# Modulation steps moved from the input projection and the heads to the output projection of the mLSTM mixer, and the first head's scores ahead of the gate rows

## The reference, cut to what matters

```python
mod = silu(c) @ ada_w[i] + ada_b[i]              # 1024 -> 6144, for each layer
u = x * (1.0 + sc_m) + sh_m
xm, z = split(u @ w_in, 2)                       # 1024 -> 2 x 2048
xc = silu(causal_depthwise_conv(xm, conv_w, conv_b))
q, k, v = block_diag_proj(xc, wq), block_diag_proj(xc, wk), block_diag_proj(xm, wv)
gates = q @ wg_q + k @ wg_k + v @ wg_v + b_gates
h = mlstm(q, k, v, i_pre, log_sigmoid(f_pre))    # 4 heads of 512, causal scores with decay
h = (norm(h) * norm_w + skip * xc) * silu(z)
y = h @ w_out                                    # 2048 -> 1024
x = layer_norm(ALPHA * x + (1.0 + g_m) * y, ...)
```

## Time and profile before

| quantity | value |
|---|---|
| time, median of 3 runs | 2680.66 us (2680.2 to 2684.01) |
| the profiled execution's own time | 2685.28 us |
| its span, first to last instruction | 2683.5 us |
| mean granted TensorE clock | 0.993 |
| busy: PE, PEld, DVE | 2607.1, 1850.0, 897.3 us |
| busy: ACT, POOL | 418.4, 909.4 us |
| HBM read | 557.75 MB, 208 GB/s over the span |

### The profile page before, as it was taken

One profiled execution on the slowest core, in us unless ns is written; L12 is line 12 of the kernel. 1 busy time (PEld: TensorE's weight loads), 2 busy tenths in 40 slices (PEclk: granted clock), 3 DMA queues, 4 the chain that ended last, 5 costly groups with the idle time before them and its releaser, 6 DMA issues.

```text
span 2683.5 us, 47152 instructions
## 1 busy us (share of the span) xinstructions
PE 2607.1 (97%) x20611; PEld 1850.0 (69%) x20611; DVE 897.3 (33%) x1623; ACT 418.4 (16%) x864; POOL 909.4 (34%) x715
## 2 busy tenths in 40 slices
PE   8999999989999999999999999999999999999998
PEld 6767899947544444444445446488888888998998
DVE  5746431483300011100013494232221136533651
ACT  0032100120311000100003244110000031221000
POOL 2672178583000000000000360145555341622886
PEclk9999999999999999999999999999999999999999
DMA  9968544477499999999997210332222243123552
GB/s 300 342 237 298 142 166 166 151 282 256 164 382 407 408 384 385 394 399 406 383 388 269 75 47 10 102 110 88 85 87 87 79 141 110 49 78 97 171 166 87
DMA packets 318304, 561.88 MB, mean 209 GB/s; under 512 B 45545, under 2 KB 181521, under 8 KB 317969
## 3 DMA queue, kind: packets, MB, share of 16 engines
q1 hardware_dynamic: 299280, 554.57, 57.9%
q10 hardware_dynamic: 18816, 4.27, 0.8%
HBM read 557.75 MB, written 1.05 MB: 208 GB/s over the span
## 4 chain that ended last, share of the span: by engine, by line
PE 50%; issue 37%; POOLq 5%; POOL 4%; DVE 2%; ACT 1%; DMA 1%; DVEq 1%; SPq 0%; ACTq 0%
PE psum L1943 10%; PE psum L2230 5%; PE psum L2019 5%; PE psum L2053 3%; PE psum L1406 3%; PE psum L1021 3%; PE psum L2295 2%; PE psum L1359 2%; PE psum L2113 2%; PE psum L1768 2%; POOLq L3906 2%; PE psum L1419 1%; PE psum L2140 1%; POOLq L4046 1%; PE psum L1062 1%
## 5 line engine op out<-in xcount | busy, mean ns | idle before, releaser
L1629 PE MATMUL psum<-ring,xe 128*32 128x512 f32 (+1 forms) x4608 | 457.8, 557 | 1.0 <-issue 1.0
L1629 PEld LDWEIGHTS psum<-ring,xe 128*32 128x32 f32 x4608 | 156.7, 110 | 289.7 <-issue 254.8
L4045 POOL TENSOR_TENSOR ckv<-ckv,nstat 128x512 f32<-128x512 f32 x2 | 2.5, 1262 | 889.6 <-DVE nstat L3548 889.6
L3438 DVE TENSOR_TENSOR act_in<-act_in,psum 128x256 f32<-128x256 f32 (+1 forms) x72 | 28.7, 399 | 628.5 <-ACT act_in L2585 628.5
L1651 PE MATMUL psum<-ring,zs 128*32 128x256 f32 x4224 | 232.3, 379 | 0.3 <-DMA ring<-in_moe_w 0.3
L1651 PEld LDWEIGHTS psum<-ring,zs 128*32 128x32 f32 x4224 | 141.5, 110 | 93.0 <-issue 5.6
L4058 POOL TENSOR_TENSOR w_sums<-ring 128x512 f32<-128x512 f32 (+1 forms) x34 | 42.3, 1245 | 293.8 <-DVE ctxT L3605 124.1
L2585 ACT ACTIVATE act_in<-psum 128x256 f32<-128x256 f32 (+1 forms) x72 | 26.3, 366 | 566.7 <-PE psum L1629 566.7
L1768 PE MATMUL psum<-a,ring 128*128 128x512 f32 x224 | 96.8, 593 | 2.0 <-ACT a L2640 1.3
L3548 DVE RECIPROCAL nstat<-nstat 128x512 f32<-128x512 f32 x23 | 75.8, 3329 | 42.1 <-ACT nstat L2337 42.1
L1021 PE MATMUL psum<-a,ring 128*128 128x256 f32 x384 | 84.4, 380 | 0.4 <-DVE a L3806 0.3
(11 more groups left out here) (616 smaller groups left out, 4858.0 us busy)
## 6 DMA issues: line engine op xcount, KB each, us to landing
ring<-in_moe_w SPq DMA_DIRECT2D x216, 1024.0 KB, 11.2
ring<-in_ffn_w SPq DMA_DIRECT2D x97, 1024.0 KB, 5.2
ring<-in_ada_w SPq DMA_DIRECT2D x96, 1024.0 KB, 8.7
ring<-in_moe_w SPq DMA_DIRECT2D x64, 768.0 KB, 6.5
ring<-in_hg_w_in SPq DMA_DIRECT2D x20, 1024.0 KB, 5.1
ring<-in_mlstm_w_in SPq DMA_DIRECT2D x16, 1024.0 KB, 8.4
ring<-in_mlstm_w_out SPq DMA_DIRECT2D x8, 1024.0 KB, 7.5
ring<-in_s_w_glu SPq DMA_DIRECT2D x8, 1024.0 KB, 11.7
```

The source lines that it names most:

```text
L1629: last = pe.matmul(psum[rows, r, 0:2 * nb * 32].rearrange("p (u b f) -> p u b f", u=2, b=nb), xe[:, k, at:at + 32], tile[:, :, :, rows], s ...
```

## The change

The number of modulation steps beside the input tiles falls from 10 to 8 (tiles 5 to 12), so tiles 13 to 15 follow each other. Eight steps, 8 to 15, stand between there and the end of the heads (ten before): one behind the q and k products, one behind the first two gate rows, two in each of the first two heads, one in each of the last two. The last four, 16 to 19, stand behind the first four tiles of the output projection, and their loads between those tiles' loads. `ada_columns` moves behind the fifth output tile.

The first head's scores move ahead of the gate columns and rows. The gate rows of heads 2 and 3 move behind the first head's values, and ACT instead of DVE copies the rows of heads 1 to 3 out. ACT's last gate exponential moves ahead of the last two copies of v. On DVE `head_scale(h)` moves from the end of head h + 1 to behind the scores of head h + 2, and both last ones stand after the loop. `s5_loads` on ACT now follows `mod_rows_out("b")`. The hunks that only renumber banks are left out:

```diff
-UNDER_INPUT, FIRST_INPUT = 10, 6
+UNDER_INPUT, FIRST_INPUT, UNDER_OUTPUT = 8, 6, 4
...
-TILES += [(f"ada_b{UNDER_INPUT}", 20), ("m_out", 8), ("ffn0", 3 * FSTEPS), ("ada_c", 28), ("glu", 8), ("ada_r", 8),
+TILES += [(f"m_in{_j}", 1) for _j in range(FIRST_INPUT + UNDER_INPUT, INPUT_TILES)]
+TILES += [(f"ada_b{UNDER_INPUT}", 16)]
+for _s in range(UNDER_OUTPUT):
+    TILES += [(f"m_out{_s}", 1), (f"ada_out{_s}", 2)]
+TILES += [("m_out_rest", 8 - UNDER_OUTPUT), ("ffn0", 3 * FSTEPS), ("ada_c", 28), ("glu", 8), ("ada_r", 8),
...
-        ("m_v", 8), ("m_cT", 1), ("m_rows", NH), ("m_head", 4 * NH),
+        ("m_v", 8), ("m_head", 5 * NH + 1),
...
+        def head_job(kind, h):
+            later = 4 * h + 5 if h else 0
+            return job_of["m_head"] + {"scores": later, "cT": 1, "rows": (2, 3, 7, 8)[h], "sums": later + 1 if h else 4,
+                                       "values": later + 2 if h else 5}[kind]
...
-    for s in range(UNDER_INPUT, ADA_STEPS["b"]):
+    for s in range(UNDER_INPUT, ADA_STEPS["b"] - UNDER_OUTPUT):
...
-    t0 = tile_of["m_out"]
...
-        load_cols(t0 + j, w["mlstm_w_out"][0], 256 * (j % 4), 256, k0=8 * (j // 4))
+        load_cols(out_tile(j), w["mlstm_w_out"][0], 256 * (j % 4), 256, k0=8 * (j // 4))
+        if j < UNDER_OUTPUT:
+            ada_b(ADA_STEPS["b"] - UNDER_OUTPUT + j)
...
-    ada_step("b", UNDER_INPUT + 1, 1)
...
-    j = job_of["m_cT"]
+    def head_scores(h):
+        j = head_job("scores", h)
+        wait_free(pe, j)
+        for s in range(2):
+            for c in range(HC):
+                last = pe.matmul(key_block(bank(j), s), xc[:, h * HC + c, s * P:(s + 1) * P],
+                                 qk[:, h * HC + c, 0, s * P:T], start=c == 0, stop=c == HC - 1)
+        full(last, j)
+    def head_rows(h):
+        j = head_job("rows", h)
+        wait_free(pe, j)
+        full(pe.matmul(bank(j), ident[0:NH, h:h + 1].broadcast_to([NH, P]),
+                       gate_rows[0:NH, 5:7].rearrange("p a t -> p (a t)"), start=True, stop=True), j)
+    wait_out(pe, job_of["m_qk"] + IC - 1)
+    head_scores(0)
+    j = head_job("cT", 0)
...
-    for h in range(NH):
-        j = job_of["m_rows"] + h
-        wait_free(pe, j)
-        full(pe.matmul(bank(j), ident[0:NH, h:h + 1].broadcast_to([NH, P]),
-                       gate_rows[0:NH, 5:7].rearrange("p a t -> p (a t)"), start=True, stop=True), j)
+    for h in range(2):
+        head_rows(h)
+    ada_step("b", UNDER_INPUT + 1, 1)
...
-    wait_out(pe, job_of["m_qk"] + IC - 1)
...
-        j = job_of["m_head"] + 4 * h
-        wait_free(pe, j)
-        for s in range(2):
-            for c in range(HC):
-                last = pe.matmul(key_block(bank(j), s), xc[:, h * HC + c, s * P:(s + 1) * P],
-                                 qk[:, h * HC + c, 0, s * P:T], start=c == 0, stop=c == HC - 1)
-        full(last, j)
-        ada_step("b", UNDER_INPUT + 2 + 2 * h, 1)
+        if h:
+            head_scores(h)
+        ada_step("b", UNDER_INPUT + 2 + min(2 * h, h + 2), 1)
...
-        wait_out(pe, j)
-        wait_free(pe, j + 1)
+        j = head_job("sums", h)
+        wait_out(pe, head_job("scores", h))
+        wait_free(pe, j)
...
+        if h == 0:
+            for later in range(2, NH):
+                head_rows(later)
...
-        ada_step("b", UNDER_INPUT + 3 + 2 * h, 1)
-    ada_columns("b", 0, 1)
+        if h < 2:
+            ada_step("b", UNDER_INPUT + 3 + 2 * h, 1)
...
-            t, j = tile_of["m_out"] + 4 * half + g, job_of["m_out"] + g
+            t, j = out_tile(4 * half + g), job_of["m_out"] + g
...
-            elif g == 1:
-                head_var(NH - 1)
+                if g == 0:
+                    ada_columns("b", 0, 1)
+            else:
+                if g == 1:
+                    head_var(NH - 1)
+                ada_step("b", ADA_STEPS["b"] - UNDER_OUTPUT + g, 1)
...
+        if g == 6:
+            act.wait_ge(S("m_sum_ready"), 1)
+            act.activation(gate_rows[0:NH, 6], gate_rows[0:NH, 6], ACT.Exp, scale=-1.0).then_inc(S("gate_rows_ready"), 1)
...
-    act.wait_ge(S("m_sum_ready"), 1)
-    act.activation(gate_rows[0:NH, 6], gate_rows[0:NH, 6], ACT.Exp, scale=-1.0).then_inc(S("gate_rows_ready"), 1)
+    def rows_out(h):
+        j = head_job("rows", h)
+        wait_full(act, j)
+        out_of(act.activation(nm[:, h], bank(j).rearrange("p (k t) -> p k t", k=2), ACT.Copy), j)
...
+        if h == 0:
+            for later in range(1, NH):
+                rows_out(later)
...
-    mod_rows_out("b")
...
+    mod_rows_out("b")
...
-    for h in range(NH):
-        j = job_of["m_rows"] + h
-        wait_full(dve, j)
-        out_of(dve.tensor_copy(nm[:, h], bank(j).rearrange("p (k t) -> p k t", k=2)), j)
...
+        j = head_job("rows", h)
+        if h == 0:
+            wait_full(dve, j)
+            out_of(dve.tensor_copy(nm[:, h], bank(j).rearrange("p (k t) -> p k t", k=2)), j)
+            dve.drain()
+        else:
+            wait_out(dve, j)
...
+    decays(0)
...
-    decays(0)
...
+        if h >= 2:
+            head_scale(h - 2)
...
-        if h:
-            head_scale(h - 1)
+    head_scale(NH - 2)
+    head_scale(NH - 1)
...
-    head_scale(NH - 1)
```

More of the change, by code:

```diff
@@ L518, in ada_tile @@
             if stage == "b":
-                return tile_of[f"ada_b{s}"] if s < UNDER_INPUT else tile_of[f"ada_b{UNDER_INPUT}"] + 2 * (s - UNDER_INPUT)
+                if s < UNDER_INPUT:
+                    return tile_of[f"ada_b{s}"]
+                at_output = s - (ADA_STEPS["b"] - UNDER_OUTPUT)
+                return tile_of[f"ada_out{at_output}"] if at_output >= 0 else tile_of[f"ada_b{UNDER_INPUT}"] + 2 * (s - UNDER_INPUT)
             if stage == "c" and s >= ADA_BATCH["c"]:
@@ L1341, in stage_mlstm @@
                                 at = h * DH + (2 * g + e) * P
-                                last = pe.matmul(bank(j + 2 + g)[:, e * T + s * P:(e + 1) * T], vbuf[:, s, at:at + P],
+                                last = pe.matmul(bank(j + g)[:, e * T + s * P:(e + 1) * T], vbuf[:, s, at:at + P],
                                                  key_block(scor[:, h % 2], s), start=s == 0, stop=s == 1,
                                                  skip_group_check=True)
-                        full(last, j + 2 + g)
+                        full(last, j + g)
+                    if h == 0:
+                        for later in range(2, NH):
+                            head_rows(later)
                     if h:
                         head_var(h - 1)
-                    ada_step("b", UNDER_INPUT + 3 + 2 * h, 1)
-                ada_columns("b", 0, 1)
+                    if h < 2:
+                        ada_step("b", UNDER_INPUT + 3 + 2 * h, 1)
                 for half in range(2):
@@ L2446, in head_squares @@
             def head_squares(h):
-                wait_out(act, job_of["m_head"] + 4 * h + 3)
+                wait_out(act, head_job("values", h) + 1)
                 act.activation(hsq, hT[:, h * HC:(h + 1) * HC], ACT.Square).then_inc(S("h_sq_ready"), 1)
@@ L3125, in stage_mlstm @@
                     out_of(dve.scalar_tensor_tensor(scor[:, h % 2], bank(j)[:, 0:CAUSAL], DH ** -0.5, decay, ALU.mult, ALU.mult), j)
-                    wait_full(dve, j + 1)
-                    dve.tensor_tensor(recip_[:, 0], bank(j + 1)[:, 0:T], nm[:, h, 1], ALU.max)
+                    if h >= 2:
+                        head_scale(h - 2)
+                    j = head_job("sums", h)
+                    wait_full(dve, j)
+                    dve.tensor_tensor(recip_[:, 0], bank(j)[:, 0:T], nm[:, h, 1], ALU.max)
                     dve.drain()
-                    out_of(dve.scalar_tensor_tensor(recip_[:, 0], bank(j + 1)[:, 0:T], -1.0, recip_[:, 0],
-                                                    ALU.mult, ALU.max), j + 1)
+                    out_of(dve.scalar_tensor_tensor(recip_[:, 0], bank(j)[:, 0:T], -1.0, recip_[:, 0],
+                                                    ALU.mult, ALU.max), j)
                     dve.drain()
@@ L3134, in stage_mlstm @@
                     dve.drain()
+                    j = head_job("values", h)
                     for g in range(2):
-                        wait_full(dve, j + 2 + g)
+                        wait_full(dve, j + g)
                         out_of(dve.tensor_tensor(hT[:, h * HC + 2 * g:h * HC + 2 * g + 2],
-                                               bank(j + 2 + g).rearrange("p (a t) -> p a t", a=2),
-                                               recip_[:, 1:2].broadcast_to([P, 2, T]), ALU.mult), j + 2 + g)
+                                               bank(j + g).rearrange("p (a t) -> p a t", a=2),
+                                               recip_[:, 1:2].broadcast_to([P, 2, T]), ALU.mult), j + g)
                     if h + 1 < NH:
```

12 lines of the change are left out of this document (7 added, 5 removed).

## The result

| | before | after |
|---|---|---|
| median, us | 2681.73 (6 runs, 2679.05 to 2685.09) | 2693.74 (5 runs, 2692.29 to 2694.27) |
| profiled execution, us (span) | 2685.28 (2683.5) | 2693.82 (2691.9) |
| ratio, 95% interval | | 1.0042 [1.0031, 1.0052] |

One more execution of the change took 4688 us at a granted clock of 0.634, and is left out. The change is slower by 12.0 us by the medians and by 8 to 14 us by the interval; the forecast was 2674.2 us, and its range ended at 2679.0.

What follows compares the result with a forecast made beforehand. PE, busy 2607.1 of 2683.5 us, was taken as the bound, leaving only waits and half-clock time to win: 3.7 + 0.74 + 0.74 - 0.5 + 1.8 = 6.5 us, so 2680.7 - 6.5 = 2674.2 us, range 2669.5 to 2679.0.

Steps and rivals of the forecast that it cites:

- the last sentence on the output projection: Output projection: the next stage's small loads follow later on ACT, but are needed only in that stage; no cost.
- The rival on the slower side: Output projection starves: its tiles, slowed to 208 GB/s, make PE wait 14.5 us; 2688.7 us, chance 0.04.
- input projection, 7.86 less two steps: Input projection: both waits for POOL's weight sums go, and tiles beside steps no longer run longer; gain 3.7 us.
- zero product to output projection, columns and their wait taken out: Gate rows and heads: gain 0.74 us at the exponential, cost 0.5 for DVE and POOL, gain 1.8 on the clock.
- columns without the copy's wait: Modulation columns, moved behind the output projection's fifth tile, no longer wait for ACT's copy of the rows; gain 0.74 us.
- output projection with steps between its tiles: Output projection: steps 16 to 19 keep PE busy as in the heads and transfers keep up; no extra cost.
- to the layer norm: All terms together: gain 6.5 us, with the layer norm beginning at about 298.4 us instead of 304.80.
- the zero product: Sign: the first product behind the input tiles comes at about 159.2 us instead of 166.59.
- the gate rows' 0.74: Gate rows: PE no longer waits for ACT's exponential behind the values; gain 0.74 us.
- DVE and POOL ahead of the output projection: End of the heads: the output projection waits for DVE and POOL; cost 0.5 us, between 0 and 1.5.
- The forecast of the clock: Gate rows and first scores: a 5.2 us half-clock loss becomes two spells of 1.7 us; gain 1.8 us.
- the rival without a spell: Gate rows: no half-clock spell is left, all 5.2 us come back; -9.9 us, 2670.8 us, chance 0.22.

Runs made afterwards that it cites:

- experiment 2: The change with the time steps loaded as whole rows of 256 bytes (128 packets instead of 4,096): 2678.05 us, 0.9984.
- experiment 3: The change with time steps loaded as whole rows, plus both transfers of 4-byte packets as loads that nobody reads: 2696.05 us, 1.0044.
- experiment 4: The change with time steps loaded as whole rows, plus one of the two 4-byte-packet transfers as an unread load: 2677.96 us, 0.9977.
- `b_rows`: The kernel before the change, with the time steps loaded as whole rows: 2684.07 us, 0.9997.
- `b_loads_later`: The kernel before the change, its nine small loads held back on ACT until PE begins the output projection's fifth tile: 2692.54 us, 1.0038.
- experiment 7: The change with time steps as whole rows, and two moved modulation steps put back under the input projection: 2679.16 us, 0.9982.
- experiment 8: The change with time steps as whole rows, and the nine small loads issued ahead of ACT's copy of the modulation rows: 2695.81 us, 1.0058.
- experiment 6: Two kernels with time steps loaded as whole rows: the kernel before, 2684.07 us, 0.9997; the change once more, 2678.9 us, 0.9985.

## Why the prediction was wrong

**The step that failed** is the last sentence on the output projection: "`s5_loads` follow later on ACT, but are needed only in the next stage." It was costed at nothing. It asked who reads the data, and when; it did not ask what the transfers do to others while they run, nor how long they run. Both could be read in the trace of before: in the kernel before the two time-step loads take up to 46.4 us from issue to landing, and a stretch of 14 us has a DMA share of 0.06 with tiles of the ring issued. In the change the same packets went out 12.7 us later and PE came 7.8 us earlier, so that they were still running when PE stopped in the middle of a group: 12.7 us of stop and 2.2 at half clock (experiments 2, 3 and 4). The term of the sum that stood at 0 was a cost of 14.9 us. The rival on the slower side, a starved output projection, named the meeting of small loads and tiles, and ruled it out since the small loads "cannot meet these tiles". They met the last ones, but with the opposite effect: the tiles reached PE in time, with no wait for DMA there, and it was the small loads that were pushed back (12.27 us on the third).

**The other terms** came out near their sizes in this pair of executions. Between marks of the two traces, with the moved steps taken out at the prediction's own 1.85 us each:

| term | forecast | measured |
|---|---|---|
| input projection, 7.86 less two steps | +3.7 | +4.2 |
| zero product to output projection, columns and their wait taken out | +2.0 | +3.7 |
| columns without the copy's wait | +0.74 | +0.85 |
| output projection with steps between its tiles | 0 | -0.9 |
| to the layer norm | 6.5 | 7.8 |

The second row is 247.74 - 166.59 = 81.15 us before, less two steps and the columns with their wait (1.66), 75.8, against 230.82 - 158.73 = 72.1. The fourth is 297.00 - 230.82 = 66.2 us against 304.80 - 247.74 = 57.1, of which four steps are 7.4 and the columns 0.8.

- Input: both waits for POOL went from the last tiles, the zero product stood at 158.73 where 159.2 was forecast.
- The second term is the gate rows' 0.74, DVE and POOL ahead of the output projection (forecast 0.5, measured 0.78), and the clock. One spell came where two were taken: a window around it reads

```profile
185.00:190.00 5.00, 5.00 (x24) 1.17 (x26) 3.31 (x7) 1.28 (x3) 4.83 (x5) 0.66 0.10 11
```

(1 - 0.66) x 5 = 1.7 us lost. It lies behind the first two gate rows with no idle time of PE near it; the second pair of rows stayed at full clock. So a spell without a gap is there again, as the row from 192 to 204 us had shown it, but behind one piece, not two. The forecast of the clock, 1.8 us, came out as 5.2 - 1.7 = 3.5. The rule of the Trainium skill on idle gaps ("TensorE: Matmul & The Clock Gate", section "HAM oscillation — how this bites in real kernels") as the prediction read it would have given 5.2; the spell without a gap is no case of it.
- How much of the 3.5 is the change? The mixer's code on PE is the same in several of the kernels, so their traces are more samples of it. From 175 to 215 us the granted clock is 0.87, 0.91 and 0.96 in three executions with the order of before (before, `b_rows`, `b_loads_later`): 5.2, 3.6 and 1.6 us lost. In eight with the change's order, or two steps off it (experiment 7), it is 0.96 in three (the change, experiments 7 and 8) and 1.00 in five. So the spell is no fixed cost of the products that use 4 of 128 rows, against what the prediction took from the rows of before, and the profiled execution of before had the longest: the prediction took 5.2 us for what every execution loses, where the mean of three is 3.5. The gain by these means is 2.9 us, between the 1.8 of the forecast and the 3.5 of the pair. In the five at 1.00 the whole spell is gone, as the rival without a spell had it.
- The same holds for the lead at the layer norm. It begins at 304.80, 303.11 and 300.00 us in the three with the order of before, and at 297.00, 296.18, 296.42, 296.17 and 295.74 in the change and four executions (experiments 2, 6, 3 and 4) that differ from it only behind that point: 6.3 us apart on average, where the one pair has 7.8 and the forecast was 6.5. That the forecast of the lead is this close is in part luck, as the errors of its terms offset each other.
- The output projection's tiles take 7.10 us each beside steps, 0.07 more than before, and each step another bit at its edges: a small cost that I had set at zero, as I had counted the same thing as a gain under the input projection.

**How much of it arrives** could be told only with the small packets gone: about 4 us by the ratios of two comparisons, between 1.6 and 7.0 by their intervals. The forecast 6.5 lies at the upper end of that, and no version had a median near 2674.2 us. Where the rest of the lead at the layer norm goes was not followed.

## What to carry to other kernels

Moving work past a queue of small loads is not free because their data is needed late: ask how many packets they are, how long those run, and which tiles and instruction blocks are due while they do. A load whose rows are single elements with a stride can be made a load of whole rows, and picked apart by the engine that reads it anyway; it cost some 0.2 us of ACT here (0.47 us for 0.23) and took out the 12.7 us stop. And one profile is one sample: what a spell at half clock costs, and so what a change can win back, is read from several executions of the same code. And an idle time "issue" in the middle of a group of like instructions, with no data near it, is a reason to look at the instruction queue before the semaphores.

## What the runs showed of the hardware

- **4-byte packets can silence the other queues.** At 106 packets a microsecond, a share of 0.047, they left 0 GB/s for ring tiles that had been issued, and no instruction block, for 32 us and more. The Trainium skill ("DMA: Bandwidth & Descriptors", section "Queues, rings and completion order") says that each engine takes its queues in turn, packet by packet; the stretch from 300 to 332 us, with tiles waiting and one queue moving, does not show such turns. In the kernel before the ring's tiles began to move again from some 302 us, at up to 343 GB/s and later near 95, while the small packets still ran; why there and not in the change stays open.
- **An engine can run out of instructions.** PE stopped 12.69, 14.02 and 8.0 us in three kernels, without any semaphore. That packets of 16.4 KB on the queue "instruction" are what it lacked is what the runs bear out: none from 300 to 332 us in the change and in experiment 3, two in the change with whole rows, and in all three kernels with a stop PE goes on 1.4 to 3.4 us after the next one. Without harm one came 44 us after the one before (experiment 4), with a stop after some 61 us (the change); the profile does not say to which engine a block goes. The Trainium skill ("Runtime: NRT & Kernel Launch", section "Terms") gives blocks of 16 KiB for the refill of an engine's instruction memory, which agrees with the packets' size.
- **A stop of PE costs more than its length.** The granted clock fell to 0.50 while PE stood still (330 to 332 us) and was still 0.50 from 340 to 342 us, with PE busy again: 2.2 us more. Here the trace agrees with the rule of the Trainium skill ("TensorE: Matmul & The Clock Gate", section "HAM oscillation — how this bites in real kernels") that idle gaps lower the clock.
